# A matrix inverse kept in transposed form alone, and scores formed in two banks at once, in a kernel of two chunked recurrences

## What is computed

```python
def rwkv7_recurrence(r, decay, k, v, a, b):
    # S_t = S_{t-1} diag(w_t) + (S_{t-1} a_t) b_t^T + v_t k_t^T,  y_t = S_t r_t
    def step(state, inp):
        r_t, w_t, k_t, v_t, a_t, b_t = inp
        sa = jnp.einsum('bhij,bhj->bhi', state, a_t)
        state = (state * w_t[:, :, None, :] + sa[..., None] * b_t[:, :, None, :]
                 + v_t[..., None] * k_t[:, :, None, :])
        y_t = jnp.einsum('bhij,bhj->bhi', state, r_t)
        return state, y_t
```

```python
    kk = jnp.einsum('bhnid,bhnjd->bhnij', kc, kc)
    lower = jnp.eye(c) + jnp.where(strict, bc[..., :, None] * kk * decay, 0.0)
    sol = lax.linalg.triangular_solve(lower, rhs, left_side=True, lower=True, unit_diagonal=True)
```

## Time and profile before

| | before |
|---|---|
| median of the runs, us | 2922.65 (2920.97 to 2925.04) |
| the profiled execution, us | 2918.25 |
| its span, us | 2916.0 |
| mean granted TensorE clock | 0.962 of 2.4 GHz |
| TensorE matmul busy | 2693.7 us (92%) |
| TensorE weight loads busy | 2163.4 us (74%) |
| VectorE busy | 1557.8 us (53%) |
| ScalarE busy | 1045.6 us (36%) |
| GpSimd busy | 449.5 us (15%) |
| first recurrence, loop over four chunks | from 316.00 to 513.46 us |
| second recurrence, loop over four chunks | from 1607.45 to 1754.90 us |

### The profile page before, as it was taken

One profiled execution on the slowest core, in us unless ns is written; L12 is line 12 of the kernel. 1 busy time (PEld: TensorE's weight loads), 2 busy tenths in 40 slices (PEclk: granted clock), 3 DMA queues, 4 the chain that ended last, 5 costly groups with the idle time before them and its releaser, 6 DMA issues. The chain is left out here.

```text
span 2916.0 us, 33247 instructions
## 1 busy us (share of the span) xinstructions
PE 2693.7 (92%) x13118; PEld 2163.4 (74%) x13118; DVE 1557.8 (53%) x2209; ACT 1045.6 (36%) x1584; POOL 449.5 (15%) x359
## 2 busy tenths in 40 slices
PE   6898999889899999978988998899998988899997
PEld 4677899667678888756777996687786765687776
DVE  3745665454546663265334664676734245567643
ACT  4653322533433322234423343422223346422222
POOL 4544434001010000000000442000021031300002
PEclk9999899889999999999998999999999999999999
DMA  4424000432123333222230001122233210222231
GB/s 141 151 83 148 2 1 1 148 97 97 53 65 101 101 93 93 90 68 64 82 107 6 1 2 51 58 91 90 86 110 98 93 58 9 66 93 90 91 105 61
DMA packets 82626, 222.09 MB, mean 76 GB/s; under 512 B 13293, under 2 KB 29950, under 8 KB 81284
## 3 DMA queue, kind: packets, MB, share of 16 engines
q1 hardware_dynamic: 78112, 205.49, 22.3%
q10 hardware_dynamic: 4360, 14.49, 1.4%
HBM read 213.60 MB, written 11.58 MB: 77 GB/s over the span
## 5 line engine op out<-in xcount | busy, mean ns | idle before, releaser
L230 DVE TENSOR_TENSOR w_low<-w_raw,w_high 128x1024 fp32r<-128x1024 f32 (+2 forms) x338 | 407.2, 1206 | 878.2 <-ACT w_high L220 878.1
L292 PE MATMUL bank<-x_high,w_high 128*128 128x512 f32 x1840 | 743.2, 404 | 46.5 <-DVE x_low L486 20.4
L293 PE MATMUL bank<-x_low,w_high 128*128 128x512 f32 x1840 | 734.3, 399 | 0.0
L294 PE MATMUL bank<-x_high,w_low 128*128 128x512 f32 x1840 | 732.4, 398 | 0.0
L220 ACT ACTIVATE w_high<-w_raw 128x1024 fp32r<-128x1024 f32 (+2 forms) x380 | 386.2, 1019 | 624.0 <-PE bank L294 501.2
L292 PEld LDWEIGHTS bank<-x_high,w_high 128*128 128x128 f32 x1840 | 349.0, 190 | 157.2 <-issue 60.5
L293 PEld LDWEIGHTS bank<-x_low,w_high 128*128 128x128 f32 x1840 | 349.3, 190 | 88.3 <-issue 5.5
L294 PEld LDWEIGHTS bank<-x_high,w_low 128*128 128x128 f32 x1840 | 349.1, 190 | 83.2
L292 PE MATMUL bank<-f_high,w_high 128*128 128x512 f32 x528 | 208.7, 395 | 0.9 <-DVE w_low L230 0.9
L294 PE MATMUL bank<-f_high,w_low 128*128 128x512 f32 x528 | 209.2, 396 | 0.0
L293 PE MATMUL bank<-f_low,w_high 128*128 128x512 f32 x528 | 209.1, 396 | 0.0
(11 more groups left out here) (607 smaller groups left out, 4236.5 us busy)
## 6 DMA issues: line engine op xcount, KB each, us to landing
w_raw<-in_ffn_in_dram SPq DMA_DIRECT2D x132, 512.0 KB, 3.4
w_raw<-in_ffn_out_dram SPq DMA_DIRECT2D x48, 512.0 KB, 3.5
w_raw<-in_gdn_in_dram SPq DMA_DIRECT2D x24, 512.0 KB, 3.4
w_raw<-in_mix_in_dram SPq DMA_DIRECT2D x22, 512.0 KB, 3.5
w_raw<-in_ffn_out_dram SPq DMA_DIRECT2D x24, 384.0 KB, 3.1
w_raw<-in_swa_qk_dram SPq DMA_DIRECT2D x12, 512.0 KB, 3.5
bias_rows<-bias_row ACTq DMA_DIRECT2D x4, 1280.0 KB, 14.7
w_raw<-in_mix_gate_a_dram SPq DMA_DIRECT2D x8, 512.0 KB, 3.5
```

The source lines that it names most:

```text
L230: (on or self.nc.vector).tensor_tensor(self.low[c % SPLIT][:, 0:w], self.raw[c % RAW][:, 0:w], self.high[c % SPLIT][:, 0:w].bitcast(F32), ...
L292: nc.tensor.matmul(out, wh, high[:, k, :], start=first + at == 0, stop=False)
L293: nc.tensor.matmul(out, wh, low[:, k, :], start=False, stop=False)
L294: last = nc.tensor.matmul(out, wl, high[:, k, :], start=False, stop=first + at == depth - 1)
```

## The change

Three things, in both recurrences unless said otherwise.

1. **The inverse.** `b` no longer forms TT^T W1. It forms only W1^T TT; VectorE adds it to TT; then TensorE transposes TT (`turn_inverse`, against the identity) into bank 3g+1 and ScalarE copies that into T (`inverse`), which sets `t_ready`. Group 0 is turned after b(1) and ahead of slot 3, group 1 behind slot 3. Level 6 has neither, as before it had no T.
2. **Scores (first recurrence only).** The two halves of ab, ak, rk and rb are formed in one call, product by product in alternation, half 0 in bank 6 and half 1 in bank 7, with one semaphore count. They move: ab to level 4 slot 0, ak to level 4 slot 2, rk to level 5 slot 0, rb to level 6 slot 0; `rhs_inside` and `y_inside` to level 5 slot 2, `turn_first` to level 6 slot 2, `turn_ends` to level 6 slot 3.
3. **The lists of ScalarE and VectorE.** They follow the new places. On ScalarE `inverse` for both groups stands at the end of levels 1 to 5: in the first recurrence behind that level's other work, in the second ahead of `decays`, `betas`, `exponents` and `key_rows`. In the first, `values` goes ahead of the level 4 products and `matrix` into level 4. On VectorE, in the first, the masks of rk go to level 5 and of rb to level 6, ahead of the sums, and `first_level` behind the sums of levels 4 and 5; in the second the work between the two sums goes behind both.

```diff
@@ first recurrence, TensorE
-            def score(left, right, bank, half, n, done):
-                o = slice(64 * half, 64 * half + 64)
+            def scores(left, right, done):
                 for q in range(4):
-                    last = nc.tensor.matmul(PS[bank][:, chunk(q)], left[o, q, :], right[o, q, :], start=True, stop=True)
+                    for half in range(2):
+                        o = slice(64 * half, 64 * half + 64)
+                        last = nc.tensor.matmul(PS[6 + half][:, chunk(q)], left[o, q, :], right[o, q, :], start=True, stop=True)
                 last.then_inc(R[done], 1)
...
+            def score_ab(n):
+                pe.wait_ge(R["vt"], n + 1)
+                if n >= 2:
                     pe.wait_ge(R["st"], n - 1)
                 elif n:
                     pe.wait_ge(R["ket"], 1)
+                pe.wait_ge(R["btt"], n + 1)
+                pe.wait_ge(R["at"], n + 1)
+                scores(X2, LD[:, :, chunk(n)], "ab")
+
+            def score_ak(n):
+                pe.wait_ge(R["mt"], at(n, 1))
                 pe.wait_ge(R["kt"], n + 1)
+                scores(Y[:, :, chunk(n)], LD[:, :, chunk(n)], "ak")
+
+            def score_rk(n):
+                pe.wait_ge(R["mak"], at(n, 1))
                 pe.wait_ge(R["rt"], n + 1)
+                scores(Y[:, :, chunk(n)], X0, "rk_scored")
+
+            def score_rb(n):
+                pe.wait_ge(R["ri"], n + 1)
+                pe.wait_ge(R["yi"], n + 1)
+                scores(X2, X0, "rb")
...
-                if level < LEVELS - 1:
-                    for i in range(N):
-                        h = N * g + i
-                        last = nc.tensor.matmul(PS[3 * g + 1][:, chunk(i)], TT[n % 2][:, h, :], W1[:, h, :], start=True,
-                                                stop=True)
-                    last.then_inc(R["t_sums"], 1)
...
+            def turn_inverse(n, level, g):
+                pe.wait_ge(R["tt_ready"], lv(n, level, g))
+                for i in range(N):
+                    last = nc.tensor.transpose(PS[3 * g + 1][:, chunk(i)], TT[n % 2][:, N * g + i, :], C["ident"][:])
+                last.then_inc(R["t_sums"], 1)
...
                     b(n, level, 1)
+                    if level < LEVELS - 1:
+                        turn_inverse(n, level, 0)
                     beside(n, level, 3)
+                    if level < LEVELS - 1:
+                        turn_inverse(n, level, 1)
@@ first recurrence, ScalarE
+            def inverse(n, level, g):
+                act.wait_ge(R["t_sums"], tl(n, level, g))
+                nc.scalar.activation(group(T, g), wide(3 * g + 1), ACT.Copy).then_inc(R["t_ready"], 1)
...
+                    if after < NT and level == 4:
+                        values(after)
                     product(n, level, 0)
...
+                    if after < NT and level == 4:
+                        matrix(after, 0)
                     product(n, level, 1)
...
+                    if level < LEVELS - 1:
+                        for g in range(G):
+                            inverse(n, level, g)
@@ first recurrence, VectorE
             def sums(n, level, g):
-                if level < LEVELS - 1:
-                    dve.wait_ge(R["t_sums"], tl(n, level, g))
-                    nc.vector.tensor_tensor(group(T, g), group(T, g), wide(3 * g + 1), ALU.add).then_inc(R["t_ready"], 1)
                 dve.wait_ge(R["tt_sums"], lv(n, level, g))
...
-                        if level == 4:
+                        if level == 5:
                             for half in range(2):
-                                keep_ak(after, half)
-                        if level == 5:
-                            for g in range(G):
-                                first_level(after, g)
+                                keep_rk(after, half)
+                        if level == 6:
+                            for half in range(2):
+                                keep_rb(after, half)
```

More of the change, by code:

```diff
@@ L1970, in _ @@
                         if level == 3:
-                            matrix(after, 1)
                             end(after)
                             start(after)
+                        if level == 4:
+                            matrix(after, 1)
                         if level == 5:
+                            inside(after)
                             output_inside(after)
                         if level == 6:
-                            inverse_start(after, 1)
+                            for g in range(G):
+                                inverse_start(after, g)
                             for i in range(2):
                                 ends(after, i)
+                    if level < LEVELS - 1:
+                        for g in range(G):
+                            inverse(n, level, g)
             delta(NT - 1)
@@ L2370, in b @@
                     pe.wait_ge(R["tt_ready"], lv(n, level, g) - G)
-                if level < LEVELS - 1:
-                    for h, o in each(g):
-                        last = nc.tensor.matmul(PS[3 * g + 1][:, o], TT[n % 2][:, h, :], W1[:, h, :], start=True, stop=True)
-                    last.then_inc(R["t_sums"], 1)
                 for h, o in each(g):
@@ L2377, in b, with turn_inverse @@
                 last.then_inc(R["tt_sums"], 1)
+            def turn_inverse(n, level, g):
+                pe.wait_ge(R["tt_ready"], lv(n, level, g))
+                for h, o in each(g):
+                    last = nc.tensor.transpose(PS[3 * g + 1][:, o], TT[n % 2][:, h, :], C["ident"][:])
+                last.then_inc(R["t_sums"], 1)
             def beside(n, level, slot):
@@ L2489, in product, with inverse @@
                 nc.scalar.activation(W1[:, a:b, :], wide(3 * g), ACT.Copy).then_inc(R["w_ready"], 1)
+            def inverse(n, level, g):
+                a, b = heads[g]
+                act.wait_ge(R["t_sums"], tl(n, level, g))
+                nc.scalar.activation(T[:, a:b, :], wide(3 * g + 1), ACT.Copy).then_inc(R["t_ready"], 1)
             def delta(n, g):
```

109 lines of the change are left out of this document (34 added, 75 removed).

## The result

The changed kernel takes 2888.8 us (median of four runs, 2887.46 to 2892.49); the kernel before, beside it, 2922.87 (2920.97 to 2925.04). The ratio is 0.9886 (95% interval 0.987 to 0.9902), 34 us less. I had forecast 2919.2, from 2908 to 2929.

A forecast was written before the change was run, and what follows sets the result against it. TensorE's issue was taken to bound both recurrences' loops. From the profiled 2918.25 us, preparation +1.4, first recurrence -2.0, -3.8 and -1.3, second +2.3 and clock 0 gave 2914.9; moved to the median 2919.2, range 2908 to 2929.

The forecast's parts named there:

- The bound and the chain: Levels with nothing beside them: a group's chain of 5.18 us, not the 4.43 of issue, bounds them; 5.42 becomes 5.18.
- rival 1: Both recurrences: chain stays hidden, TensorE remains the bound in every level; worth 17.8 + 13.3 + 2.6 - 1.4 = 32: 2890; 4%.
- The price of a score: First recurrence: a whole score takes 2.35 us, pairs 0.225 apart, so side by side gains only 2.6 us.
- Rival 2: Score pairs run side by side at full clock: a score costs 1.29, times 12 gives 13 us less: 2906; 8%.
- Level 1 of the middle chunks: First recurrence: transposes and a copy behind VectorE's late first sum make the level 7.4 us (was 6.37), +1.1.
- The inverse in the first recurrence: 40 product groups become 40 transpose groups: 17.8 us of issue saved, kept only where TensorE stays the bound.
- The preparation: Ahead of the first recurrence's loop: masks and copies waited for in pairs, transposes for a later rb; +1.4 us (0 to 2.5).
- The second recurrence: Its loop gets 2.3 us slower (bounds -3 and +6): chunk 0 +2.3, last chunk -0.4, middle chunk 40.2 against 39.99.
- the queue: Second recurrence: ScalarE's inverse copies delay next-chunk preparation; 5.0 us in a row, level 6 from 3.99 to 5.4 to 5.65.
- The clock: Both recurrences: one fall to 1.2 GHz, worth 3.2 us, goes and one comes; 0 in the sum.
- The new gaps that I named: Gaps of 1.5 to 1.8 us: level 1 of two middle chunks, levels 3 and 5 of second recurrence's chunk 0.
- rival 3: Each gap of 1.5 us or more, transposes about it, can start a 3.2 us clock fall: 2929 to 2932; 14%.

The follow-up runs named there:

- The fillers: Changed kernel with four identity transposes (0.44 us of issue) added once in each of three levels with nothing beside them, each in another slot; one execution 2891.77 us.
- everything ahead on ScalarE: Changed kernel with the second recurrence's decays, betas and key rows made group by group ahead of the same group's inverse copy; 2896.69 us, ratio 0.9921 to the kernel before.
- the run with both edits: Changed kernel with first-recurrence level 4 spread over other slots, and second-recurrence decays, betas and key rows ahead of each group's inverse copy; 2892.74 us.
- the combination: Changed kernel with level 4 spread, first_level behind rk's masks, second-recurrence betas and key rows ahead of inverse copies, decays behind; 2883.66 us, ratio 0.9888 to kernel before.

## Why the prediction was wrong, step by step

**The bound and the chain: right.** An empty level is 5.13 (5.18 forecast), the idle times stand before the second transposes and behind them, levels 2 and 3 are 6.86 and 8.90 (6.9, 8.9), the last chunk gained 1.5 (1.3). The fillers show spare time for their 0.44 at the one place where the chain has it. (The prediction's 40 x (0.89 - 0.44) is 18.0 and not 17.8, and its 0.2 x 12 is 2.4 and not 2.6; both stand in rival 1's sum, neither in the forecast.)

**The price of a score: wrong, and the largest miss.** 2.35 was taken, 1.29 is what it takes. Two errors stood in it. The pair pace of 0.225 came from a stage that reads its operands with a step; the read, not the shape, made the pace. And 0.35 for edges was added on top of a pace that already filled the time; even one after the other a score takes 1.84. With four scores in each of the first three chunks this is 2.24, 0.98 and 1.09 in levels 4, 5 and 6 of a middle chunk, 4.3 in all. Rival 2 named the mechanism and its 1.29 exactly, at 8%, and expected 13; three times 4.3 is 12.9. Of that the pairing proper is 5.8, the rest is halves in turn that I charged too dear. This is the step that failed most: the 0.225 came from a row of the right shape and the wrong read.

**Level 1 of the middle chunks: mis-sized.** 7.4 forecast, 6.26 measured, twice 1.1. VectorE's rows in chunk 2, before and then after:

```profile
423.04 1.64 DVE L1994 TENSOR_TENSOR x<-x,x 128x512 f32<-128x512 f32 x1
424.61 1.76 DVE L1997 TENSOR_TENSOR x<-x 128x512 f32<-128x512 f32 x1
...
406.98 0.68 DVE L1985 TENSOR_TENSOR x<-x 128x512 f32<-128x512 f32 x1
407.69 1.70 DVE L1987 TENSOR_TENSOR x<-x,x 128x512 f32<-128x512 f32 x1
...
409.32 0.68 DVE L1990 TENSOR_TENSOR x<-x 128x512 f32<-128x512 f32 x1
...
411.25 0.42 PEld L1778 LDWEIGHTS bank<-ident,tt 128*128 128x128 f32 x4 [0.31 <-DVE tt L2049]
```

Only one of the four exponents is slowed beside GpSimd (1.70), where two were before (1.64 and 1.76); GpSimd's masks, one block from 422.49 to 425.82 before, now are two, 407.58 to 408.85 and 409.37 to 411.15. The fourth exponent runs beside the second of these and is not slowed, and why is open. The transposes issue 4.92 into the level, not at 6.0. I moved VectorE's work by 0.4 and left its durations, though one of them depended on the moment.

**The inverse in the first recurrence** is worth 10.0 of 17.8 at equal clock. The forecast didn't give it alone; its levels 2 and 3 show that the step was sound. Rival 1 came within 1.2 us of the time by luck, by three terms that are each wrong (17.8, 13.3 and 2.6, measured 10.0, under 2 and 14.0 in the loop with the slots).

**The preparation: hit by luck.** +1.4 forecast, +1.7 measured. The sum had waits of 0.6 each. The runs show 5.9 by new slots and whole scores, up to 3.4 of it the clock, and 4.0 back by pairing; the sum had neither.

**The second recurrence: sign wrong, the queue right in kind and too dear.** +2.3 forecast, -1.7 measured. Middle levels 7.08, 7.36, 7.92, 6.01, 5.83, 4.90 against 7.13, 7.54, 7.99, 5.99, 6.03, 5.5. Level 6 was the worst. I added ScalarE's work there to 5.0 in a row, each group of three key or value rows and each copy behind the end of the one before. In the trace each starts before the last one ends, and the row lasts 4.35:

```profile
1655.17 1.65 ACT L2459 ACTIVATE k_rows<-bank,tail 128x128 f32<-128x128 f32 x6
...
1658.91 0.60 ACT L2479 ACTIVATE t<-bank 128x384 f32<-128x384 f32 x1
```

The six key rows are 0.36 to 0.40 long and start 0.25 apart, so the next product copy starts 1.50 after the first of them, where I had 1.76. The level ends 0.6 earlier. The Trainium skill, ScalarE: Activation LUTs, What ACT_TABLE_LOAD costs, has ACTIVATEs in a row overlap by some 93 ns; these key rows overlap by 0.11 to 0.15, and the value rows and copies behind them by up to 0.22. Chunk 0 was 35.63 against 37.5, by smaller stalls in levels 2 and 3 (6.19 and 5.71 against 6.6 and 6.5).

**The clock: count wrong.** I let one fall go and one come. None came in either loop in the two traces of the changed kernel. The fall in the kernel before, worth 3.2, isn't in its second trace; that it went by the shorter stall (0.75 in place of 1.71) fits the three falls behind eight stalls of 1.70 to 1.75, but isn't shown. The new gaps that I named were shorter than the 1.5 to 1.8 forecast: level 1 of the middle chunks is idle for 0.15 in all, level 3 of the second recurrence's chunk 0 for 1.22 and level 5 for 1.37. No fall follows the last two in any trace that has them (9 and 13):

```profile
1600.90 1.60 PE L2363 MATMUL bank<-tt,w 128*128 128x128 f32 x12 [1.22 <-ACT w L2486]
```

Yet with everything ahead on ScalarE gaps of 1.02 are followed by a fall in chunks 0 and 2 and by none in chunk 1, and so again in the run with both edits, four of six. So rival 3's mechanism exists, but the length of a gap doesn't say where, and the transposes that now stand about every gap brought no more falls.

**What stays open** is the rest of the 34 us. In traces without a fall in the loops the two recurrences with what lies around them became 24 us shorter (first: 231.3 to 207.7; second: 167.0 to 166.5; the second trace of before against the first of after). The stretch between the two, the same code in all, lasted 1063.9 and 1071.2 us in two traces of the kernel before, 1066.7 and 1063.1 in two of the changed one, and 1073.1 and 1069.8 in the two with the old inverse in the first recurrence. In all twelve traces with the new inverse there it is 1063.1 to 1067.7. It differs by where the clock falls. Whether the shorter first recurrence shifts that in its favour, as the medians and these stretches hint, these runs don't settle.

## What to carry to other kernels

Take a price from a row only if the row has the same reads as well as the same shape: a step in an operand doubled the time of a pair. When a chain replaces issue, add its steps with the queue places in which work beside is free; that held to 0.05 us. And on an in-order engine, put ahead of a critical copy only what is ready: betas and key rows paid, decays that wait for another engine cost 1.3 in their level and gave only 0.6 back in the next. Last, where traces gain less than the times scatter, compare kernels beside each other: the combination gained 8.2 us in its loops and nothing that shows in its ratio.

## What the runs showed of the hardware that was not expected

- Two fp32 passes of 64 rows on different halves of the partitions start 0.11 apart as a pair at 2.4 GHz, so sixteen take 1.10 us; read with a step of four fp32 in either operand, 0.22 to 0.23.
- With all of one half ahead of the other in the list, sixteen passes still take 1.64 us and not 16 x 0.11 = 1.76 and an edge: in the trace the second half's first passes start between the last ones of the first half, some only 0.004 to 0.006 behind.
- At half clock the pairing brought 4.0 us in the preparation alone (32.97 to 28.98), four scores.
- A stall of 1.70 to 1.75 us was followed by a fall of the clock in three of its eight appearances, in one of four within the two traces of the kernel before; gaps of 1.02 by four of six, gaps of 1.22 and 1.37 by none of 22.
